# Seven products instead of eight in the last chunk of each MLP, and a new order around it

## What is computed

```
def squared_relu_mlp(x, w_up, w_down):          # w_up 1024 x 4096, w_down 4096 x 1024
    return jnp.square(jax.nn.relu(x @ w_up)) @ w_down

x = layer_norm(ALPHA * x + mixer(x), ln1_g[i], ln1_b[i])
x = layer_norm(ALPHA * x + squared_relu_mlp(x, w_up[i], w_down[i]), ln2_g[i], ln2_b[i])
```

## Time and profile before

| | us |
|---|---|
| median of 3 runs (lowest, highest) | 1097.0 (1096.88, 1097.88) |
| profiled execution, its own time | 1098.72 |
| its span, first to last instruction | 1096.9 |
| TensorE busy | 1076.7 (98%) |
| VectorE busy | 802.6 (73%) |
| ScalarE busy | 562.0 (51%) |
| GpSimd busy | 163.7 (15%) |
| mean granted TensorE clock | 0.996 |

### The profile page before, as it was taken

One profiled execution on the slowest core, in us unless ns is written; L12 is line 12 of the kernel. 1 busy time (PEld: TensorE's weight loads), 2 busy tenths in 40 slices (PEclk: granted clock), 3 DMA queues, 4 the chain that ended last, 5 costly groups with the idle time before them and its releaser, 6 DMA issues.

```text
span 1096.9 us, 22319 instructions
## 1 busy us (share of the span) xinstructions
PE 1076.7 (98%) x8535; PEld 1054.7 (96%) x8535; DVE 802.6 (73%) x1264; ACT 562.0 (51%) x995; POOL 163.7 (15%) x200
## 2 busy tenths in 40 slices
PE   8999999999999999999999999999999999999996
PEld 7999999999999999999999878999999999999996
DVE  6999899896758568566874574789958668586666
ACT  5999857652433425333666775665533424235233
POOL 2343042000000000011243564300000000000023
PEclk9999999999999999999999999999999999999998
DMA  7323224031413314173041221130423403234202
GB/s 248 115 87 97 74 63 136 19 116 58 136 40 133 117 36 134 44 245 101 20 135 45 61 59 38 48 108 1 154 65 110 134 24 129 72 101 135 77 1 82
DMA packets 63709, 98.66 MB, mean 90 GB/s; under 512 B 4384, under 2 KB 44768, under 8 KB 63616
## 3 DMA queue, kind: packets, MB, share of 16 engines
q1 hardware_dynamic: 62944, 94.81, 27.4%
q0 software_dynamic: 400, 2.21, 0.5%
q10 hardware_dynamic: 288, 0.59, 0.2%
HBM read 95.06 MB, written 3.56 MB: 90 GB/s over the span
## 4 chain that ended last, share of the span: by engine, by line
PE 80%; DVE 10%; ACT 4%; issue 2%; DMA 1%; POOL 1%; SPq 0%; DVEq 0%; ACTq 0%; POOLq 0%
PE bank L1921 10%; PE bank L1922 9%; PE bank L1923 9%; PE bank L2166 8%; PE bank L2168 8%; PE bank L2167 8%; PE bank L2140 6%; PE bank L2142 6%; PE bank L2141 6%; PE bank L1999 2%; PE bank L2001 2%; PE bank L2000 2%; DVE w_lo L1107 2%; PE bank L2275 1%; PE bank L2300 1%
## 5 line engine op out<-in xcount | busy, mean ns | idle before, releaser
L1114 DVE TENSOR_TENSOR w_lo<-stage,w_hi 128x1024 fp32r<-128x1024 f32 x120 | 144.8, 1219 | 56.1 <-ACT w_hi L648 56.1
L648 ACT ACTIVATE w_hi<-stage 128x1024 fp32r<-128x1024 f32 x120 | 124.4, 1054 | 112.5 <-DVE stage L1132 64.7
L1921 PE MATMUL bank<-x_hi,w_hi 128*128 128x288 f32 (+1 forms) x560 | 163.9, 293 | 1.4 <-issue 0.6
L1922 PE MATMUL bank<-m_lo,w_hi 128*128 128x288 f32 (+1 forms) x560 | 162.2, 290 | 0.0
L1922 PE MATMUL bank<-x_lo,w_hi 128*128 128x288 f32 (+1 forms) x560 | 161.7, 289 | 0.0
L1921 PE MATMUL bank<-m_hi,w_hi 128*128 128x288 f32 (+1 forms) x560 | 161.6, 289 | 0.0
L1923 PE MATMUL bank<-m_hi,w_lo 128*128 128x288 f32 (+1 forms) x560 | 161.6, 289 | 0.0
L1923 PE MATMUL bank<-x_hi,w_lo 128*128 128x288 f32 (+1 forms) x560 | 160.9, 287 | 0.0
L2140 PE MATMUL bank<-m_hi,w_hi 128*128 128x288 f32 (+1 forms) x512 | 147.7, 289 | 0.3 <-DVE m_lo L1457 0.3
L2142 PE MATMUL bank<-m_hi,w_lo 128*128 128x288 f32 (+1 forms) x512 | 147.6, 288 | 0.0
L2141 PE MATMUL bank<-m_lo,w_hi 128*128 128x288 f32 (+1 forms) x512 | 147.4, 288 | 0.0
(11 more groups left out here) (271 smaller groups left out, 2792.4 us busy)
## 6 DMA issues: line engine op xcount, KB each, us to landing
stage<-w_up SPq DMA_DIRECT2D x64, 512.0 KB, 4.4
stage<-w_down SPq DMA_DIRECT2D x64, 512.0 KB, 3.7
stage<-w_qkv SPq DMA_DIRECT2D x10, 512.0 KB, 4.0
stage<-w_x SPq DMA_DIRECT2D x8, 512.0 KB, 5.2
stage<-w_y SPq DMA_DIRECT2D x8, 512.0 KB, 3.6
stage<-w_out SPq DMA_DIRECT2D x8, 512.0 KB, 3.7
stage<-w_o SPq DMA_DIRECT2D x8, 512.0 KB, 3.8
y_t<-acc SPq DMA_DIRECT2D x4, 288.0 KB, 2.4
```

The lines of the kernel that those rows point to most:

```text
L648: A(hi, raw, ACT.Copy).then_inc(s_whi, 1)
L1114: vt.tensor_tensor(lo, raw, hi.bitcast(F32), ALU.subtract).then_inc(s_wlo, 1)
L1921: mm(out, wh, xh, start=(k == 0), stop=False)
L1922: mm(out, wh, xl, start=False, stop=False)
```

## The change

The last chunk (`CHUNKS - 1`) of each MLP is made like the six before it, with seven products, in an order of its own. The hardware loop makes one pass more and covers chunk 6. TensorE's list for the last chunk becomes: P1, P2, P6, P5, P3, down of the first half, P7, norm sums of the first half, P4, down of the second half with the weight rows in the order 2, 3, 0, 1. VectorE and ScalarE get lists of their own for it (`last_up`, `last_square`, `last_chunk`). The banks of the last chunk and of the next stage are named by hand. The sums of the first half's norm move into memory that the token sums no longer use. At the end of layer 1 the outputs of the odd tiles of the first half move from GpSimd to ScalarE, and GpSimd's loads of the attention cache in layer 0 start after the last chunk's P3 instead of after chunk 6's first down half.

```diff
-            plan(("last", l), "A" * 4 + "V" * 8 + "A")
-            plan(("ln", 2 * l + 1, 0), "AV")
-            plan(("last_rest", l), "A" * 3 + "V" * 8)
+            b = [(len(reader) + k) % BANKS for k in range(BANKS)]
+            plan(("last", l), "AA-VAAAA-V" + "V" * 8 + "-V",
+                 b[6:8] + b[2:4] + b[6:8] + b[4:6] + b[4:6] + b[0:6] + b[0:2] + b[6:8])
+            plan(("ln", 2 * l + 1, 0), "AV", b[2:4])
+            plan(("last_p4", l), "-A", b[6:8])
+            plan(("last_rest", l), "V" * 8, b[4:6] + b[0:2] + b[6:8] + b[2:4])
+            return b[4:6] + b[0:4] + b[6:8]
...
+            def last_chunk(l):                      # ScalarE
+
+                c, L = CHUNKS - 1, 2 * l + 1
+                t0 = (CHUNKS * l + c) * 8
+                for t in range(2):
+                    keep(l, c, 0, P1, t, h11[:, t, :])
+                split_in(l, c, T3, product_done(l, c, P1))
+                split_in(l, c, B22, product_done(l, c, P2))
+                for t in range(2):
+                    keep(l, c, 0, P6, t, h12[:, t, :])
+                split_in(l, c, T4, product_done(l, c, P6))
+                hidden(l, c, 0, 0, 0, 0, (s_hsq, t0 + 4))
+                for t in range(2):
+                    keep(l, c, 0, P5, t, h22[:, t, :])
+                for k in DOWN:
+                    split_in(l, c, k, down_unit(l, c - 1, 1, 7) + 1)
+                hidden(l, c, 0, 1, 2, 0, (s_hsq, t0 + 6))
+                for m in range(KT):
+                    square(L, 0, m)
+                norm_mean(L, 0)
+                hidden(l, c, 0, 3, 2, 1, (s_hsq, t0 + 8))
+                norm_root(L, 0)
+                act.wait_ge(s_unit, product_done(l, c, P4))
+                b0 = bank_of(product_unit(l, c, P4))
+                A(h21[:, :, :], bank[:, b0:b0 + 2, 0:HW], ACT.Relu).then_inc(s_evA, 1)
+                hidden(l, c, 0, 2, 0, 1, (s_hsq, t0 + 10))
+                gj = job_at[("qkv", 0)][0]
+                if l == 0:
+                    split([gj])
+
+                def beside(t):
+                    if l == 0:
+                        if t >= 2:
+                            square(L, 1, 2 * t - 4)
+                            square(L, 1, 2 * t - 3)
+                    else:
+                        for m in ((0, 1, 2, 3), (4,), (5, 6, 7), ())[t]:
+                            square(L, 1, m)
+
+                norm_apply(L, 0, beside)
+                if l == 0:
+                    for m in range(4, KT):
+                        if m < KT - 1:
+                            split([gj + m - 3])
+                        square(L, 1, m)
...
+            def last_up(l):                         # VectorE
+
+                c = CHUNKS - 1
+                split_in(l, c, T3)
+                combine(l, c, 0, P2, h11[:, :, :], P1)
+                relu_sq(l, c, 0, h11[:, :, :], P2)
+                split_in(l, c, B22)
+                hidden_lo(l, c, 0, 0, 0, 0)
+                split_in(l, c, T4)
+                split_in(l, c, D0)
+                split_in(l, c, D1)
+                combine(l, c, 0, P3, h12[:, :, :], P6)
+                relu_sq(l, c, 0, h12[:, :, :], P3)
+                split_in(l, c, D2)
+                split_in(l, c, D3)
+                hidden_lo(l, c, 0, 1, 2, 0)
+
+            def last_square(l):
+
+                c = CHUNKS - 1
+                dve.wait_ge(s_evA, read_by(product_unit(l, c, P4, 2), "A"))
+                vt.scalar_tensor_tensor(h21[:, :, :], h21[:, :, :], 0.0, h21[:, :, :], ALU.max, ALU.mult)\
+                    .then_inc(s_hsq, 2)
...
-                up(l, 4, CHUNKS - 1)
+                last = CHUNKS - 1
+                combine(l, last, 0, P7, h22[:, :, :], P5)
+                relu_sq(l, last, 0, h22[:, :, :], P7)
                 norm_stats(L, 0)
+                hidden_lo(l, last, 0, 3, 2, 1, 2)
                 gj = job_at[("qkv", 0)][0]
 
-                def ups(t):
...
+                def beside_centre(t):
+                    if t == 1:
+                        last_square(l)
+                    if t == 2:
+                        hidden_lo(l, last, 0, 2, 0, 1, 3)
+
+                def beside_mult(t):
+                    if l:
+                        for m in ((0, 1, 2, 3), (4,), (5, 6, 7), ())[t]:
+                            add_tile("down", L, 1, m)
+                    elif t == 3:
+                        add_tile("down", L, 1, 0)
+                        add_tile("down", L, 1, 1)
+                        split([gj])
+
+                def beside_low(t):
+                    if l:
+                        return
+                    if t == 0:
+                        add_tile("down", L, 1, 2)
+                        add_tile("down", L, 1, 3)
+                    if t in (1, 2):
+                        add_tile("down", L, 1, 3 + t)
+
+                norm_apply(L, 0, beside_low, beside_mult, centred=beside_centre)
+                if l == 0:
+                    for m in (6, 7):
+                        split([gj + m - 5])
+                        add_tile("down", L, 1, m)
+                    split([gj + 3])
...
-            pool.wait_ge(s_unit, down_unit(0, CHUNKS - 2, 0, 7) + 1)
+            pool.wait_ge(s_unit, product_done(0, CHUNKS - 1, P3))
...
-                for k in range(4):
-                    pe.wait_ge(s_hlo, i * 8 + (t0 + k + 1))
-                    if h == 0 and 0 < c < CHUNKS - 1:
+                for n, k in enumerate((2, 3, 0, 1) if h and c == CHUNKS - 1 else range(4)):
+                    pe.wait_ge(s_hlo, i * 8 + (t0 + n + 1))
+                    if h == 0 and c:
...
-                up(l, last, 0, w0)
+                for p in (P1, P2, P6, P5, P3):
+                    upward(l, last, p, w0)
                 down(l, last, 0, w0)
-                up(l, last, 1, w0, ts=(0,))
+                upward(l, last, P7, w0)
                 norm_sums(2 * l + 1, 0)
-                up(l, last, 1, w0, ts=(1, 2, 3))
+                upward(l, last, P4, w0)
                 down(l, last, 1, w0)
```

More of the change, by code:

```diff
@@ L314, in build @@
         plan_tiles("o", 0)
-        plan_mlp(0)
-        plan(("ln", 1, 1), "AV")
-        plan(("qkv", 0, 0), "AAAA")
-        plan(("qkv", 1, 0), "AAAA")
-        ab = [(mark[("qkv", 0, 0)] + k) % BANKS for k in range(BANKS)]
+        ab = plan_mlp(0)
+        plan(("ln", 1, 1), "AV", ab[6:8])
+        plan(("qkv", 0, 0), "AAAA", ab[0:4])
+        plan(("qkv", 1, 0), "AAAA", ab[4:8])
         PV, FILL, SCORE, TRANS = (ab[0], ab[3]), ab[1:3], ab[4:6], ab[6:8]
@@ L382, in plan_mlp_jobs @@
             st0 = turn[0] % STAGES
-            for c in range(1, CHUNKS - 1):
+            for c in range(1, CHUNKS):
                 ring[0] = w0 + 8 * c
@@ L1607, in mlp @@
                 chunk_down(l, 1)
[L1608 removed]
+                with dve.Fori(0, CHUNKS - 3) as i:
                     chunk_up(l, 2, i)
                     chunk_down(l, 2, i)
[L1611 to L1617 removed]
@@ L1643, in mlp @@
-                for m in range(4, KT):
-                    add_tile("down", L, 1, m)
-                    if l == 0 and m > 4:
-                        split([gj + m - 4])
+                def beside_centre(t):
[11 more added lines that the diff above has]
+                        split([gj])
@@ L1810, in add_square @@
                 pos = tile_pos(L, h, m)
-                s2 = sums[h][1]
-                squares = sqt_late if L == 2 else sqt
+                s2 = sums_of(L, h)[1]
+                squares = square_tiles(L, h)
                 pool.wait_ge(s_sqt, pos + 1)
```

271 lines of the change are left out of this document (112 added, 159 removed).

## The result

The changed kernel takes 1106.18 us (median of 4 runs, 1104.61 to 1106.41), the kernel before 1096.94 us beside it (1096.87 to 1097.88): ratio 1.0075, 95% interval 1.0063 to 1.0087. It is slower by 9.2 us in the medians and by 6.9 to 9.5 us in the interval of the ratio; the forecast was 1103.9 (6.9 us slower), range 1098.7 to 1107.5. The forecast's 6.9 us lies at the lower end of that interval.

What follows compares the result with a forecast made beforehand. TensorE was taken to set the time, with the change's worth depending on VectorE handing over in time. Layer 0's 5.2 us and layer 1's 1.7 were added to 1097.0, giving 1103.9 us, range 1098.7 to 1107.5.

Steps and rivals of the forecast that it cites:

- The third weight row: Down half one, each last chunk: TensorE waits 3.1 us for h12's low part, from +17.7 to +20.8; bounds 2.8 to 4.
- Behind it: Rest of each last chunk: P7 ends +32.5, P4 waits 0.3 us, chunk ends +49.6 against +49.13; costs TensorE 0.5 us.
- (b): Rival: the clock falls to half rate after four TensorE gaps, losing 1 to 1.5 us each; 1109 us; chance 0.10.
- the two waits that I had announced there: Layer 0's qkv group: TensorE waits for the second weight slab's split, then GpSimd's square sum, together about 5 us.
- The queue of VectorE, layer 0: Behind the norm sums: 26.2 us of VectorE work, +32.7 to +58.9; next norm sum at +60.75, 5.2 us late.
- Layer 1: Layer 1's tail: last tile addition at +51.0 instead of +49.33, 1.7 us late; bounds 0.5 and 2.7.
- Sum: Whole kernel: 5.2 us in layer 0 plus 1.7 in layer 1, 6.9 us slower, giving 1103.9 us.
- (a): Rival: only TensorE's waits count while VectorE and GpSimd keep up, 0.5 us per layer; 1098.0 to 1099.5 us; chance 0.14.
- (c): Rival: weight rows D2 and D3 land later beside the cache loads, another 1 to 2 us in layer 0; 1105.5; chance 0.08.
- (d): Rival: TensorE stays full to each chunk's end, so 48 fewer matmuls save 5.65 us; 1091.4 us; chance 0.06.

Runs made afterwards that it cites:

- e1: The changed kernel with h12's high copy and low part put ahead of weight row D3's split in the last chunk: 1102.14 us, ratio 1.0044.
- e2: The changed kernel with 24 matmuls of unused result filling TensorE's gap ahead of the third weight row: 1106.0 us.
- e9: The changed kernel with GpSimd's square additions for layer 0's second half over 8 of 288 columns (not computing the function): 1105.4 us.
- e3: The changed kernel with VectorE's running sums of layer 0's second half, tiles 1 to 7, over 8 of 288 columns (not computing the function): 1108.37 us.
- e5: The changed kernel with GpSimd's attention cache loads starting after the last chunk's first down half instead of after P3: 1117.6 us.
- e12: e10 with VectorE's running sums and GpSimd's square sums of both layers' second halves over 8 of 288 columns (not computing the function): 1096.17 us, ratio 0.9993.
- e11: e10 with the first half's norm sums placed between the two columns of P7 instead of behind both: 1103.2 us.
- e6: e1 with two qkv slabs' low parts moved to GpSimd in layer 0, and layer 1's second-half tiles added before the last three root products: 1105.8 us.
- e8: e6 with layer 0's second-half norm sums asked after six input tiles, and P7 ahead of down half one, P4 ahead of first-half norm sums: 1102.7 us.
- e10: e1 with layer 0 reordered: qkv slab copies and second slab split earlier, second-half norm sums after six input tiles, nothing added to GpSimd: 1101.6 us.

## Why the prediction was right, and what it mis-sized

**The third weight row.** Predicted asked at +17.7, ready at +20.8, wait 3.1 us. Measured: last matmul before it at +17.8, restart at +20.7 and, in layer 1, +20.7; idle 2.62 and 2.55. e1 shows the cause that I gave, the place of D3's split ahead of h12's low part: 1.5 of the 2.6 us. The other 1.1 are mostly the splits of D0 and D1 in front of P3's sum; my sum had them in it, ending at +16.0, but I did not name them as a cause.

**Behind it.** In layer 1 the norm sums began at +32.5 (predicted P7's end +32.5), the wait before P4 was 0.3 to 0.4, and the chunk ended at about +50.0 (+49.6).

**The clock.** This is the first mis-sized term. I gave the fall behind a gap to rival (b), at 1 to 1.5 us for each of four gaps, and nothing in the sum. Layer 0 fell behind its gap and paid 1.5 us (e2), layer 1 did not; the tail paid 0.7. The fall in the qkv group (0.85 and 0.81) was free: TensorE came to the norm sum at 557.47 and GpSimd was done only at 557.83. What counts is the fall at the third row: the norm sums of layer 0 were at +34.1 instead of +32.5, and everything behind them 1.6 us late. The fall in the qkv group hid the second of the two waits that I had announced there: only the one for the slab shows, 3.42 us, where I had about 5 in two; e1, at full clock, has both (3.4 and 1.0).

**The queue of VectorE, layer 0.** Predicted 26.2 us of work from +32.7 to +58.9. Measured from 529.26 (+34.3) to 556.03 (+61.1), 26.8 us. The next norm sum at +62.99 instead of +60.75 is the clock's 1.6 and 0.6 of the queue. The sum held, but I had taken it for VectorE's alone. e9 shows that 1.8 us of these 26.8 is time lost beside GpSimd; most of it entered my sum unseen through durations of the kernel before, where the same collisions happen, as in this low part of x, which takes 0.69 us elsewhere:

```profile
543.02 1.30 DVE L1405 TENSOR_TENSOR x_lo<-acc,x_hi 128x512 fp32r<-128x512 f32 x1
```

The 0.6 us more are one weight split, 1.21 us before and 1.81 beside GpSimd in the change. e3 shows GpSimd's chain as close a limit as VectorE's.

**Layer 1.** Last tile addition predicted +51.0, measured 1090.49, +51.3: 2.0 us late where 1.7 was predicted.

**Sum.** Predicted 5.2 + 1.7 = 6.9; measured 7.4 + 2.2 + 0.7, less the 0.1 between the norms, 10.2 in the profiled stretch and 9.2 in the medians.

**The rivals.** (a) is out: VectorE and GpSimd do not keep up (3.42 us in the qkv group, 1.30 in layer 1). (b) was half true, as above. The Trainium skill ("TensorE: Matmul & The Clock Gate", HAM oscillation) describes the clock falling at every wait, in a kernel whose waits are longer than the bursts of matmuls between them. Here the bursts are longer, so the page does not by itself lead to (b), as I had written; the clock fell behind half of the gaps at the third row. The one gap of before that I set against the warning was too little evidence: in e5 a shorter one at the same place (2.31 us before 13.06) was followed by clock 0.50 from 14.5 to 17.5. (c) is out by e5. (d), the other side, needed both the third row and the queue; with half of the third row's wait and nearly all of the queue's gone, e12 stands at 1.0 us less, not 5.65.

**Open.** No version that computes everything has a median below 1101.6 us. With four runs of most versions and one profile of each, differences of 1.5 us and less between versions are not settled. Whether another split of the weights in the last chunk could bring D2 earlier wasn't tried, nor was the change in one layer alone.

## What to carry to other kernels

Fewer matmuls are worth nothing where TensorE's time is another engine's cover: add up that engine's list from the event that releases it to the event that the next stage wants, and compare it with the matmuls left between. Before you move work to an idle engine, look at what its operations do to those beside them; and before you move a wait or an event, name what stands behind it in its list (e5) and what it has been covering (e11).

## What was unexpected of the hardware

- Additions of 128x288 on GpSimd took 0.80 or 0.81 us alone and up to 1.86 beside VectorE's operations with two SBUF operands, and slowed these too: a weight split 1.22 to 1.81 us, a low part of x 0.68 to 1.28. With 8 columns instead of 288 (e9) all five splits took 1.22. Two GpSimd subtractions (2.69 us each) made four products of 0.69 us take 5.1 instead of 2.5 (e6), and four subtractions of 0.68 us take 6.9 instead of 2.7 (e8).
- The length of a gap in a busy TensorE did not settle whether the clock fell. Of eight gaps of 2.37 to 2.65 us at the third row (the change, e3, e5, e9, two layers each) it fell behind four (0.50 to 0.67 in the stretches after them): layer 0 in the change, layer 1 in e3, e5 and e9. In the qkv group it held behind 3.40 us in e1 (1.00 from 550 to 555) and fell behind 3.42 in the changed kernel; it held behind 2.32 us in e10 and fell behind 2.32 in e11 (0.50 from 554.2 to 557.4) and behind 1.84 in e9 (0.50 from 552 to 555). At the third row it held behind all of 1.5 us or less.
